# High and low parts of the weight chunks interleaved word by word in one tile

## The chip, the cores and the metric

The kernel runs on one core of one Trainium2 chip. The metric is the device time of one execution in microseconds (us). A core has TensorE (PE in the rows: matmuls; PEld: the loads of its stationary operand, the weights), VectorE (DVE), ScalarE (ACT), GpSimd (POOL) and SyncE (SP), which issues most of the transfers. The engines run on their own instruction streams and meet at semaphores.

## The reference, cut to what matters

One layer of a decoder for 256 prompt positions and 8 sample positions that share the weights, in float32:

```
h = RMSNorm(x);  [qA,kA,vA,qB,kB,vB] = h @ w_in              # 2048 -> 4352
oA = sliding window attention, oB = dilated window attention
x += RMSNorm(concat(RMSNorm(oA), RMSNorm(oB)) @ w_out)       # 2048 -> 2048
h = RMSNorm(x)
u = h @ w_gate;  up = h @ w_up                               # 2048 -> 5632, twice
y = (gelu(causal_conv3(u)) * up) @ w_down                    # 5632 -> 2048
x += RMSNorm(y)
```

The products with the five weight matrices matter here. They read 190.8 MB of weights once.

## The kernel before, in words

The 264 positions (`TOK`) lie along the free dimension, the features along the 128 partitions. Weights are the stationary operand and arrive in 364 chunks of 128 x 1024 floats (512 KB): 68 of `w_in`, 32 of `w_out`, 176 of `w_gate` and `w_up`, 88 of `w_down`. Everything goes through a ring of four slots (`RING`):

- SyncE loads chunk n into `raw[:, slot]` (`load`, line 360), once chunk n - 4 has been split by VectorE.
- ScalarE copies it to `wh[:, slot]` (`split`, line 424). The tile has the type fp32r, so this cast rounds to the high part. It waits for the chunk, and until TensorE is done with chunk n - 4.
- VectorE writes the low part, `wl = raw - wh` (`split`, line 681), once the cast is done.
- TensorE multiplies. `mm3` (lines 1130 to 1132) makes each product of three matmuls: high weight by high activation, high weight by low activation, low weight by high activation. Each has 128 stationary columns and 264 moving columns, and each loads its weights anew. A chunk has eight such products, 24 matmuls. `gemm` calls `mm3` for `w_in`, `w_out`, `w_gate` and `w_up`, `down` for `w_down`.

The activations are split in the same way: `hh` and `hl`, in the attention stage also `oBh` and `oBl`, for the last product `gh` and `gl`. They are the moving operand.

The order of work is written out by hand. In the attention stage (chunks 0 to 83) a table `PLAN` sets the attention's steps between the chunks: scores, masks, exponentials, transposes (line 1219) and products. Then comes the second half of `w_out`, then a loop over 22 rounds of 8 chunks for `w_gate` and `w_up`, called the FFN loop here: TensorE fills two banks with `u` and two with `up`; VectorE moves `u` to `U` (lines 912 and 913), subtracts chunks, adds the taps of the convolution (line 922), takes `up` (line 937), multiplies (940) and makes `gl` (943); ScalarE makes the first tap, the gelu (635 and 636) and `gh` (640). The last stage runs over `w_down` in two halves of 44 chunks. The first chunk is cast and split in two halves (lines 563 and 566, 849 and 853), so that TensorE can begin earlier.

Of the kernel before, what the change touches and what calls it, by code (L numbers as in the profile page):

```python
# [22 lines left out]
F32R = mybir.dt.float32r  # L23
# [4 lines left out]
P = 128  # L28
# [13 lines left out]
CH = 1024  # L42
RING = 4
# [146 lines left out]
def build(nc, d):  # L190

    ctx = ExitStack()
    with ctx:
# [3 lines left out]
        def sb(name, shape, dt=F32, into=ctx):  # L197
            return into.enter_context(nc.sbuf_tensor(name, shape, dt))
# [1 line left out]

        xT = sb("xT", [P, MT, TOK])
        raw = sb("raw", [P, RING, CH])
        wh = sb("wh", [P, RING, CH], F32R)
        wl = sb("wl", [P, RING, CH], F32R)
        par = sb("par", [P, N_PAR])
        ident = sb("ident", [P, P])
        ones = sb("ones", [P, P])
# [1351 lines left out]
```

## Time and profile before

| | |
|---|---|
| three timed runs | 1193.79, 1193.95, 1194.48 us, median 1193.95 |
| profiled execution, its own time | 1196.02 us |
| its span, first to last instruction | 1194.2 us |
| mean granted TensorE clock | 0.992 of full |
| busy: TensorE, weight loads | 98%, 95% |
| busy: VectorE, ScalarE, GpSimd | 58%, 46%, 9% |
| read from memory | 216.45 MB, 185 GB/s over the span |

Matmuls are pipelined and overlap in the records, so a matmul that "takes" 285 ns can start 122 ns after the one before. The pace of TensorE is therefore the length of a window divided by the number of matmuls in it. The weight load of a matmul runs while the matmul before it still streams. The durations of VectorE and ScalarE instructions are those of the engine's work, with a fixed part for each instruction.

### The profile page before, as it was taken

Reading aid. Unit: us, or ns where it says so; the run is one execution under the profiler, and the core shown is the slowest. Engines: PE = TensorE matmul, PEld = TensorE weight load, DVE = VectorE, ACT = ScalarE, POOL = GpSimd, SP = SyncE. Lnnn points to the kernel's source line nnn. Section 1 sums busy time; section 2 is a strip of 40 time slices with the busy share of each in tenths; the row PEclk is TensorE's granted clock in tenths of the full one; section 3 lists DMA queues with packets and bytes.
Section 4 is the critical chain, followed back from the end, with each engine's and each line's share of the span. In section 5 each row is a group of like instructions: output and inputs, shape, how many; then the busy total and the mean of one; then the engine's idle time right before and its main releaser. Section 6 shows DMA issues by size and latency. Waiting matters only on the chain.

```text
span 1194.2 us, 25575 instructions
## 1 busy us (share of the span) xinstructions
PE 1168.1 (98%) x9947; PEld 1135.4 (95%) x9947; DVE 698.4 (58%) x1050; ACT 554.4 (46%) x859; POOL 105.8 (9%) x163
## 2 busy tenths in 40 slices
PE   9999999999999799999999999999999999999995
PEld 8999889988899799999999999999999999999995
DVE  5877565674375865655656565656565444454445
ACT  7455555565455654444444443444444433343331
POOL 0100111110002010011001000100110000020001
PEclk9999999999999899999999999999999999999998
DMA  8746677676555345555465555555555655555551
GB/s 309 208 142 226 235 252 235 213 228 234 168 172 180 107 144 193 180 178 183 162 201 168 191 157 196 168 184 170 182 181 182 205 182 176 178 184 183 177 158 72
DMA packets 59473, 222.21 MB, mean 186 GB/s; under 512 B 7064, under 2 KB 7264, under 8 KB 57312
## 3 DMA queue, kind: packets, MB, share of 16 engines
q1 hardware_dynamic: 55152, 196.58, 51.2%
q0 software_dynamic: 4272, 24.94, 6.2%
q8 instruction: 35, 0.57, 0.2%
q14 instruction: 14, 0.11, 0.0%
HBM read 216.45 MB, written 5.00 MB: 185 GB/s over the span
## 4 chain that ended last, share of the span: by engine, by line
PE 93%; DVE 3%; DMA 2%; ACT 1%; issue 1%; SPq 0%; POOL 0%; DVEq 0%; ACTq 0%
PE ps L1130 29%; PE ps L1131 29%; PE ps L1132 28%; PE ps L1301 1%; DMA Vk<-in_vb 1%; PE ps L1219 1%; DVE wl L681 1%; PE ps L1282 1%; DMA xT<-in_x 1%; PE ps L1210 1%; PE ps L1208 1%; PE ps L1237 0%; PE ps L1155 0%; DVE yT L977 0%; DVE ps L976 0%
## 5 line engine op out<-in xcount | busy, mean ns | idle before, releaser
L1130 PE MATMUL ps<-hh,wh 128*128 128x264 f32 x2080 | 600.1, 289 | 8.2 <-DVE hl L886 5.8
L1132 PE MATMUL ps<-hh,wl 128*128 128x264 f32 x2080 | 593.0, 285 | 0.0
L1131 PE MATMUL ps<-hl,wh 128*128 128x264 f32 x1952 | 557.7, 286 | 0.0
L681 DVE TENSOR_TENSOR wl<-raw,wh 128x1024 fp32r<-128x1024 f32 x363 | 438.4, 1225 | 192.2 <-ACT wh L424 191.7
L424 ACT CAST wh<-raw 128x1024 fp32r<-128x1024 f32 x363 | 374.6, 1046 | 275.4 <-PE ps L1132 272.0
L1130 PEld LDWEIGHTS ps<-hh,wh 128*128 128x128 f32 x2080 | 394.0, 189 | 20.5 <-issue 17.5
L1132 PEld LDWEIGHTS ps<-hh,wl 128*128 128x128 f32 x2080 | 392.8, 189 | 0.0
L1131 PEld LDWEIGHTS ps<-hl,wh 128*128 128x128 f32 x1952 | 368.7, 189 | 0.1
L1131 PE MATMUL ps<-gl,wh 128*128 (+1 forms) x704 | 200.4, 285 | 0.0
L1130 PE MATMUL ps<-gh,wh 128*128 (+1 forms) x704 | 200.1, 284 | 0.0
L1132 PE MATMUL ps<-gh,wl 128*128 (+1 forms) x704 | 199.6, 283 | 0.0
L1130 PEld LDWEIGHTS ps<-gh,wh 128*128 128x128 f32 x704 | 132.5, 188 | 0.9 <-issue 0.9
L1131 PEld LDWEIGHTS ps<-gl,wh 128*128 128x128 f32 x704 | 132.6, 188 | 0.0
L1132 PEld LDWEIGHTS ps<-gh,wl 128*128 128x128 f32 x704 | 132.4, 188 | 0.0
L1096 POOL COPY co<-U 128x4 f32 (+1 forms) x22 | 21.2, 964 | 423.1 <-DVE U L913 423.1
L912 DVE TENSOR_TENSOR U<-ps,rB 128x512 f32<-128x512 f32 x22 | 15.2, 691 | 73.2 <-PE ps L1132 73.2
L630 ACT ACTIVATE cv<-U,par 128x280 f32<-128x280 f32 x44 | 25.0, 617 | 63.5 <-DVE U L913 63.5
L937 DVE TENSOR_TENSOR up<-ps,rB 128x528 f32<-128x528 f32 x21 | 14.9, 707 | 67.8 <-PE ps L1132 67.8
L640 ACT CAST gh<-up 128x528 f32 (+1 forms) x22 | 14.0, 634 | 73.0 <-DVE up L940 72.9
L922 DVE SCALAR_TENSOR_TENSOR cv<-U,par,cv 128x280 f32<-128x280 f32 x88 | 41.0, 506 | 9.9 <-ACT cv L630 6.8
L1130 PE MATMUL ps<-oBh,wh 128*128 128x264 f32 x128 | 37.6, 294 | 0.0
L1131 PE MATMUL ps<-hh,wh 128*128 128x264 f32 x128 | 36.5, 285 | 0.0
(229 smaller groups left out, 832.5 us busy)
## 6 DMA issues: line engine op xcount, KB each, us to landing
raw<-in_w_gate SPq DMA_DIRECT2D x88, 512.0 KB, 3.7
raw<-in_w_up SPq DMA_DIRECT2D x88, 512.0 KB, 4.6
raw<-in_w_down SPq DMA_DIRECT2D x88, 512.0 KB, 3.5
raw<-in_w_in SPq DMA_DIRECT2D x67, 512.0 KB, 4.8
raw<-in_w_out SPq DMA_DIRECT2D x32, 512.0 KB, 3.8
Kt<-in_kb POOLq DMA_DIRECT2D x8, 1284.0 KB, 6.2
Vk<-in_vb POOLq DMA_DIRECT2D x8, 1024.0 KB, 7.1
out_y<-yT SPq DMA_DIRECT2D x8, 264.0 KB, 2.1
```

The costliest lines, as they stand in the source:

```text
L424: nc.scalar.copy(wh[:, slot], raw[:, slot]).then_inc(hi_ready, 1)
L630: nc.scalar.activation(cv[:, k], U[:, k, 0:NU - 2], ACT.Identity, scale=par[:, bass.ds(i * 2 + (C_CW + k), 1)], bias=par[:, bass.ds(i * 2 ...
L640: nc.scalar.copy(gh[:, bass.ds(i * 2, 2)], up[:]).then_inc(gh_ready, 1)
L681: V.tensor_tensor(wl[:, slot], raw[:, slot], wh[:, slot].bitcast(F32), ALU.subtract).then_inc(lo_ready, 1)
L912: line.do(V.tensor_tensor(U[:, :, 2:2 + SEQ], ps[:, g:g + 2, 0:SEQ], wide(rB[:, 0:SEQ]), ALU.mult))
L922: ins = V.scalar_tensor_tensor(cv[:, k], U[:, k, tap:tap + NU - 2], par[:, bass.ds(i * 2 + (C_CW + FT * tap + k), 1)], cv[:, k], ALU.mult, ...
L937: V.tensor_tensor(up[:], ps[:, 2:4, 0:TOK], wide(rB[:]), ALU.mult).then_inc(up_taken, 1)
L1096: line.do(G.tensor_copy(co[:, bass.ds(i * 2, 2), 0:2], U[:, :, SEQ:SEQ + 2]))
L1130: nc.tensor.matmul(out, a, x, start=start, stop=False)
L1131: nc.tensor.matmul(out, a, xl, start=False, stop=False)
L1132: return nc.tensor.matmul(out, b, x, start=False, stop=stop)
L1208: nc.tensor.matmul(ps[:, B_S + h, 0:P], q[:, 0:P], k[:, 0:P], start=True, stop=True)
```

## The change

The tiles `wh` and `wl`, of four slots by 1024 words each, become one tile `whwl` with the last dimension 2, and `wh` and `wl` are now names of its even and its odd words. The tile has the bytes of the two before. All that reads or writes them stays as it is written: the casts write every second word, the subtractions read every second word and write the others, and each weight load reads 128 words, every second one of 256. `raw` and the activations stay contiguous.

```diff
--- before.py
+++ after.py
@@ -200,8 +200,8 @@
 
         xT = sb("xT", [P, MT, TOK])
         raw = sb("raw", [P, RING, CH])
-        wh = sb("wh", [P, RING, CH], F32R)
-        wl = sb("wl", [P, RING, CH], F32R)
+        whwl = sb("whwl", [P, RING, CH, 2], F32R)
+        wh, wl = whwl[:, :, :, 0], whwl[:, :, :, 1]
         par = sb("par", [P, N_PAR])
         ident = sb("ident", [P, P])
         ones = sb("ones", [P, P])
```

The instructions that touch them, before and after alike:

```python
nc.scalar.copy(wh[:, slot], raw[:, slot]).then_inc(hi_ready, 1)                       # 424
V.tensor_tensor(wl[:, slot], raw[:, slot], wh[:, slot].bitcast(F32), ALU.subtract)    # 681
a, b = wh[:, slot, c:c + P], wl[:, slot, c:c + P]                                     # mm3
```

## Rows read from the trace of the kernel before

**Rows 1.** The page: busy time by engine, and the chain that ended last.

```profile
PE 1168.1 (98%) x9947; PEld 1135.4 (95%) x9947; DVE 698.4 (58%) x1050; ACT 554.4 (46%) x859; POOL 105.8 (9%) x163
...
PE 93%; DVE 3%; DMA 2%; ACT 1%; issue 1%; SPq 0%; POOL 0%; DVEq 0%; ACTq 0%
PE ps L1130 29%; PE ps L1131 29%; PE ps L1132 28%; PE ps L1301 1%; DMA Vk<-in_vb 1%; PE ps L1219 1%; DVE wl L681 1%; PE ps L1282 1%; DMA xT<-in_x 1%; PE ps L1210 1%; PE ps L1208 1%; PE ps L1237 0%; PE ps L1155 0%; DVE yT L977 0%; DVE ps L976 0%
```

**Rows 2.** Groups by line and form: name, shapes, count, busy us, mean ns, idle before.

```profile
L681 DVE TENSOR_TENSOR wl<-raw,wh 128x1024 fp32r<-128x1024 f32 x363 | 438.4, 1225 | 192.2 <-ACT wh L424 191.7
L1130 PEld LDWEIGHTS ps<-hh,wh 128*128 128x128 f32 x2080 | 394.0, 189 | 20.5 <-issue 17.5 <-DVE wl L681 1.8 <-DVE vT L693 1.1
...
L424 ACT CAST wh<-raw 128x1024 fp32r<-128x1024 f32 x363 | 374.6, 1046 | 275.4 <-PE ps L1132 272.0 <-DMA raw<-in_w_in 2.6 <-ACT ge L650 0.3
...
L1219 PEld LDWEIGHTS ps<-ident,Sm 128*128 128x128 f32 x96 | 11.5, 140 | 0.0
...
L1301 PEld LDWEIGHTS ps<-Vk,pT 128*32 128x32 f32 x256 | 6.7, 109 | 3.5 <-DMA Vk<-in_vb 2.3 <-issue 1.2
...
L853 DVE TENSOR_TENSOR wl<-raw,wh 128x512 fp32r<-128x512 f32 x1 | 0.7, 692 | 1.1 <-ACT wh L566 1.1
...
L566 ACT CAST wh<-raw 128x512 fp32r<-128x512 f32 x1 | 0.6, 619 | 1.0 <-DMA raw<-in_w_in 1.0
```

**Rows 3.** Windows: us, busy (instructions) of each engine, granted clock, DMA share, GB/s.

```profile
36.00:200.00 164.00, 163.44 (x1545) 149.63 (x1546) 111.67 (x284) 84.63 (x197) 18.14 (x40) 1.00 0.66 214
450.00:750.00 300.00, 300.00 (x2451) 300.00 (x2451) 179.49 (x219) 132.37 (x167) 27.84 (x39) 1.00 0.55 180
850.00:1150.00 300.00, 300.00 (x2464) 300.00 (x2463) 145.31 (x141) 118.11 (x129) 14.89 (x14) 1.00 0.58 182
392.90:403.20 10.30, 5.50 (x25) 5.53 (x26) 10.13 (x16) 5.11 (x10) 0.00 (x0) 0.50 0.05 14
```

**Rows 4.** Timeline, clock at 0.5: start us, us, engine, line, tiles, count, idle before.

```profile
397.70 0.56 PE L1130 MATMUL ps<-hh,wh 128*128 128x264 f32 x1 [5.75 <-DVE hl L886]
...
398.06 0.42 PE L1131 MATMUL ps<-hl,wh 128*128 128x264 f32 x1
...
398.28 0.42 PE L1132 MATMUL ps<-hh,wl 128*128 128x264 f32 x1
```

**Rows 5.** Timeline of the weight loads around one transpose of `Sm`.

```profile
93.47 0.36 PEld L1219 LDWEIGHTS ps<-ident,Sm 128*128 128x128 f32 x3
```

**Rows 6.** Groups by form: short instructions with a step of three, and their long neighbours.

```profile
L912 DVE TENSOR_TENSOR U<-ps,rB 128x512 f32<-128x512 f32 x22 | 15.2, 691 | 73.2 <-PE ps L1132 73.2
...
L635 ACT ACTIVATE ge<-cv 128x512 f32<-128x512 f32 x22 | 13.9, 633 | 26.1 <-DVE cv L922 26.1
...
L636 ACT ACTIVATE ge<-cv 128x16 f32<-128x16 f32 x22 | 4.5, 207 | 0.0
...
L913 DVE TENSOR_TENSOR U<-ps,rB 128x16 f32<-128x16 f32 x22 | 3.7, 170 | 0.0
```

**Rows 7.** Timeline of the start.

```profile
10.30 1.23 DVE L681 TENSOR_TENSOR wl<-raw,wh 128x1024 fp32r<-128x1024 f32 x1 [0.96 <-ACT wh L424]
...
11.58 0.39 PE L1130 MATMUL ps<-hh,wh 128*128 128x264 f32 x1 [0.40 <-DVE wl L681]
```

**Rows 8.** Timeline of VectorE in one round of the FFN loop.

```profile
568.49 0.71 DVE L937 TENSOR_TENSOR up<-ps,rB 128x528 f32<-128x528 f32 x1 [3.31 <-PE ps L1132]
569.23 0.71 DVE L940 TENSOR_TENSOR up<-up,ge 128x528 f32<-128x528 f32 x1
570.92 0.71 DVE L943 TENSOR_TENSOR gl<-up,gh 128x528 f32 x1 [0.99 <-ACT gh L640]
...
580.34 0.69 DVE L912 TENSOR_TENSOR U<-ps,rB 128x512 f32<-128x512 f32 x1 [3.66 <-PE ps L1132]
580.94 0.17 DVE L913 TENSOR_TENSOR U<-ps,rB 128x16 f32<-128x16 f32 x1
...
582.58 2.01 DVE L922 SCALAR_TENSOR_TENSOR cv<-U,par,cv 128x280 f32<-128x280 f32 x4 [0.34 <-ACT cv L630]
```

## The prediction

> **What bounds the kernel now.** I read the page first, then the windows, then the groups of instructions by form, then short stretches of the timeline. TensorE is busy for 98% of the span, and the chain that ended last is 93% TensorE, with 29, 29 and 28% on the three matmul lines 1130, 1131 and 1132 [rows 1]. These are the three products of `mm3`: high weight by high activation, high weight by low activation, low weight by high activation. There are 364 chunks of 24 such matmuls, 8736 in all. VectorE is busy 58%, ScalarE 46% [rows 1], and both spend their time mostly in the two splitting instructions: the cast of a chunk, 363 times 1046 ns, and the subtraction, 363 times 1225 ns [rows 2].
>
> What the reader should take from the windows is the pace of TensorE: from 450 to 750 us it issues 2451 matmuls in 300 us, 122.4 ns each, and from 850 to 1150 us 2464, 121.8 ns each, both at the full granted clock [rows 3]. Two shorter times lie under that pace. In the one stretch with a granted clock of 0.5 (1.2 GHz, after TensorE had waited 5.75 us for `hl`), matmuls of the same form start 0.22 us apart [rows 4]; at double that clock the same 264 columns would take 0.110 us. And a weight load takes 0.83 ns a column, (189 - 109) / (128 - 32) from the loads of 128 and of 32 columns [rows 2], so 107 ns for 128; the three loads for a transpose, back to back, last 0.36 us, which at 140 ns for one [rows 2] is (0.36 - 0.14) / 2 = 0.11 us from start to start [rows 5]. So the load runs under the matmul before it and has at most some 13 ns to spare. The profile does not say which of the two makes the pace 122 instead of 110. That is the thin place of this change.
>
> **The change, part by part.** *Instructions.* None is added, removed or moved; every engine has the same instructions in the same order and the tiles take the same bytes. The sum therefore has only terms for the rate at which a step of two words (8 bytes) is read or written. The stream of matmuls that reads `hh`, `hl`, `gh`, `gl` keeps its step of one.
>
> *Weight loads, 8736 of them, on the path.* No row shows a load with a step. Lower bound of the cost: zero. The moving side of TensorE reads 264 columns of 4 bytes in at most 122.4 ns, 8.6 bytes per ns and partition, from the same memory [rows 3]. A load with a step of two passes over 128 x 8 bytes in 107 ns, 9.6 bytes per ns, words skipped included, and that is the rate of the moving side without its 12 ns (1056 bytes in 110 ns). So if the load's read path can do what the moving one does, skipped words are free. Upper bound: a column costs twice as much, 213 ns a load, and the load is then the bound: (213 - 122) x 8736 = 795 us. A gain I don't expect: the load is not shorter in any reading. I take zero, because the nearest row, the moving read, is within a few per cent of the rate needed.
>
> *Subtractions on VectorE, 363, and casts on ScalarE, 363.* The slopes are (1225 - 692) / 512 = 1.04 ns an element for VectorE and (1046 - 619) / 512 = 0.83 ns for ScalarE [rows 2]. Now the cast writes with a step of two, the subtraction reads one source and writes with it. Nearest rows: line 913 writes `U` with a step of three words, 16 elements, in 170 ns. The line through 512 elements (691 ns, line 912) at the slope above leads to 691 - 496 x 1.04 = 175 ns for 16 elements; doubled elements would add 17 ns. Line 636 on ScalarE reads `cv` with a step of three, 16 elements, in 207 ns, where 633 - 496 x 0.83 = 221 is the line [rows 6]. Neither shows a price, though 16 elements are few. Upper bound: elements cost double, 1225 + 1067 = 2.29 us and 1046 + 854 = 1.90 us. I take zero. What hides a small price: TensorE uses a chunk for 24 x 122 = 2.93 us, and the waits of the two engines are long, 191.7 us of VectorE for the cast and 272.0 us of ScalarE for TensorE [rows 2].
>
> *Start.* Up to about 20 us some casts and subtractions are themselves in the chain, for example the wait of `wl` on the cast and of TensorE on `wl` [rows 7]. At the taken price nothing changes; at double it costs about three subtractions and two casts, 3 x 1.07 + 2 x 0.85 = 5 us.
>
> Sum: 0. The profiled execution took 1196.02 us, 1194.2 of it span; the three timed runs have the median 1193.95, 2.07 less. No term gives a difference, so the forecast is that median, 1194.
>
> There is a rule that speaks against this change. The Trainium skill, "Vector Engine (DVE) Microarchitecture Reference", section 5.2, says that a port of VectorE runs at full rate only where its consecutive elements come in runs of two or more adjacent words, and gives 1.7 to 2.5 ns a column where elements hop singly. By it the subtraction would be about 1.9 to 2.7 us, an estimate. The row of line 913 speaks against it, with the shortness named. The skill's "SBUF — State Buffer", "Specifications (TRN2)", says otherwise: 16-byte lines, full bandwidth with two accesses in each, which a step of two words gives; the sum by that is zero. No run here has a long stepped access yet.
>
> **The rivals.** *VectorE pays double (slower, decided at 2.2 us a subtraction).* One round of the FFN loop is 8 chunks, 192 x 122.4 ns = 23.5 us. From a release of `U`, VectorE works 0.69 + 0.17 on `U`, 2.01 on the taps, 0.71 + 0.71 on `up`, waits 0.99 for ScalarE, 0.71 on `gl` [rows 8], 5.99 us, and eight subtractions. These fit while 8 s + 6.0 < 23.5, s < 2.19 us. With 2.29 a round takes 24.3 us: 0.8 us lost x 20 rounds = 16 us. Busy VectorE would be 179.49 + 102 x 1.07 = 289 of 300 us there, and 111.67 + 42 x 1.07 = 157 of 164 us in the attention stage [rows 3], where it also waits for scores; I put 10 us there, and 5 at the start. Together 31, so 1225. In the down stage 145.31 + 103 x 1.07 = 256 of 300 fits. For it: a wider step has to cost somewhere. Against: lines 913 and 636.
>
> *The load and the moving stream get in each other's way (slower).* The 12.4 ns between 110 and 122.4 may be stalls of reads that meet. When a load passes over twice the bytes, these can double: 12.4 x 8736 = 108 us, so 1302; a tenth of it is already 11 us. For it: the pace is above both floors and no wait explains it. Against: with three or more engines at work the pace hardly moves (122.4 with VectorE 60% busy, 121.8 with 48%).
>
> *The load pays per column (much slower).* 1194 + 795 = 1989; partial prices start to count after 13 ns a load, 12% of it. Against: the rate of the moving side.
>
> *A little faster.* The layout shifts which addresses meet, and a pace of 121.8 everywhere instead of 122.4 gives 0.6 x 5000 = 3 us, so 1191. Nothing in the profile asks for it.
>
> **How the numbers follow.** No effect 0.60 (1192 to 1196); VectorE or ScalarE pays 0.10 (1205 to 1245); reads meet 0.12 (1197 to 1302); the load pays per column 0.12 (1300 to 1990); a little faster 0.06 (1188 to 1191). The range from 1190 to 1245 leaves out the fourth case, the upper half of the third and a part of the last, 0.2 together. About 0.2%, 2.4 us, is what a measurement of this kernel can tell from no change. Same 0.60, slower 0.34, faster 0.06.
>
> **What would show it.** Right: loads of 128 columns at 189 ns, some 2451 matmuls in 300 us of the FFN, cast and subtraction at 1046 and 1225 ns. First rival: the subtraction above 2.2 us, TensorE waiting for it in the FFN loop. Second: the pace between 123 and 135 ns with loads of 189 ns. Third: loads of 230 ns and more, with the casts as before. The forecast is wrong if the step costs TensorE more than the 13 ns it can hide; no row of before can exclude that.

## The result, and the profile after

The changed kernel takes 1199.16 us, median of 20 runs; beside it the kernel before took 1193.78 us, median of 20. The ratio is 1.0042, with a 95% interval of 1.0036 to 1.0048: 5 us slower. The forecast was 1194.0 us, no change; the time lies inside the range of 1190 to 1245, on the side that had a chance of 0.34.

The profiled execution took 1199.3 us, with a span of 1197.5 us, 3.3 us more than before. Its page, the chain that ended last (compare [rows 1]):

```profile
PE 93%; DVE 3%; DMA 1%; ACT 1%; issue 1%; SPq 0%; POOL 0%; DVEq 0%; ACTq 0%
PE ps L1130 29%; PE ps L1131 29%; PE ps L1132 29%; PE ps L1301 1%; DMA Vk<-in_vb 1%; PE ps L1219 1%; DVE whwl L681 1%; PE ps L1282 1%; DMA xT<-in_x 1%; PE ps L1210 1%; PE ps L1208 1%; PE ps L1237 0%; PE ps L1155 0%; DVE yT L977 0%; DVE ps L976 0%
```

TensorE carries the chain as it did. The two splitting instructions and the loads, by line and form (compare [rows 2]):

```profile
L681 DVE TENSOR_TENSOR whwl<-raw,whwl 128x1024 fp32r<-128x1024 f32 x363 | 439.6, 1229 | 199.7 <-ACT whwl L424 199.1
L424 ACT CAST whwl<-raw 128x1024 fp32r<-128x1024 f32 x363 | 410.8, 1148 | 257.4 <-PE ps L1132 255.9 <-DMA raw<-in_w_in 0.8 <-ACT ge L650 0.3
...
L1130 PEld LDWEIGHTS ps<-hh,whwl 128*128 128x128 f32 x2080 | 407.6, 196 | 21.4 <-issue 18.7 <-DVE whwl L681 1.5 <-DVE vT L693 1.1
```

Everything that has a step of two now takes a little longer, and in very different measure. The subtraction goes from 1225 to 1229 ns. The cast goes from 1046 to 1148 ns, 10% or 0.10 ns an element. The weight load goes from 189 to 196 ns. What ScalarE waits for TensorE went down by 16 us, from 272.0 to 255.9: that is where part of its longer casts (36 us busy) went, and VectorE waits 199.1 instead of 191.7 us for them.

The windows show where TensorE lost its time (columns as in [rows 3]). First before, the one stretch of the attention stage that the prediction did not use:

```profile
60.00:180.00 120.00, 120.00 (x1146) 109.43 (x1145) 80.58 (x204) 62.38 (x146) 11.59 (x26) 1.00 0.66 215
```

The same stretches after:

```profile
60.00:180.00 120.00, 120.00 (x1141) 109.50 (x1140) 80.59 (x203) 65.99 (x149) 10.69 (x24) 1.00 0.65 211
450.00:750.00 300.00, 300.00 (x2452) 300.00 (x2451) 179.32 (x219) 142.23 (x165) 27.46 (x39) 1.00 0.54 180
850.00:1150.00 300.00, 300.00 (x2443) 300.00 (x2443) 143.95 (x140) 125.94 (x128) 14.89 (x14) 1.00 0.57 180
```

In the FFN loop the number has not changed, 2452 matmuls against 2451. In the third window there are 2443 in 300 us against 2464, 122.8 ns each instead of 121.8: 21 x 122.8 = 2.6 us lost in this window. It is not the stage of `w_down` alone: that stage begins at 921 us, so the first 71 us still belong to the FFN loop, and both means are mixed. In the attention stage 1141 stand against 1146, with a granted clock of 1.00 in both. The start times in the records say it more sharply. Count the matmuls of the program from 0. From matmul 7900 to 9600, all in the stage of `w_down`, 206.74 us became 209.09, 121.61 and 123.00 ns a matmul; from 4000 to 7600, in the FFN loop, both kernels take 441.00 us, 122.50 ns a matmul. Counted over the pairs of matmuls that follow each other without a wait in both kernels, the longer pace costs 1.3 us before the FFN loop, 0.1 or less in the FFN loop, 2.8 us in the stage of `w_down`: 4.1 us. This count comes from one pair of profiled executions, whose spans differ by 3.3 us; the medians of 20 differ by 5.4. The rest of 1.3 us is not placed.

### The profile page after: what moved, and what is told of

It reads as the page before. It is cut to its first block, busy times and chain, and to the rows that moved or that the text cites. A ratio compares the mean times of both kernels' runs of the same rounds, so it can differ in the third digit from the quotient of the medians.

```text
span 1197.5 us, 25575 instructions
## 1 busy us (share of the span) xinstructions
PE 1171.8 (98%) x9947; PEld 1139.3 (95%) x9947; DVE 699.8 (58%) x1050; ACT 590.5 (49%) x859; POOL 106.1 (9%) x163
## 4 chain that ended last, share of the span: by engine, by line
PE 93%; DVE 3%; DMA 1%; ACT 1%; issue 1%; SPq 0%; POOL 0%; DVEq 0%; ACTq 0%
PE ps L1130 29%; PE ps L1131 29%; PE ps L1132 29%; PE ps L1301 1%; DMA Vk<-in_vb 1%; PE ps L1219 1%; DVE whwl L681 1%; PE ps L1282 1%; DMA xT<-in_x 1%; PE ps L1210 1%; PE ps L1208 1%; PE ps L1237 0%; PE ps L1155 0%; DVE yT L977 0%; DVE ps L976 0%
## 5 line engine op out<-in xcount | busy, mean ns | idle before, releaser
L1130 PE MATMUL ps<-hh,whwl 128*128 128x264 f32 x2080 | 601.9, 289 | 9.0 <-DVE hl L886 5.8
L1132 PE MATMUL ps<-hh,whwl 128*128 128x264 f32 x2080 | 593.6, 285 | 0.0
L1131 PE MATMUL ps<-hl,whwl 128*128 128x264 f32 x1952 | 558.9, 286 | 0.0
L681 DVE TENSOR_TENSOR whwl<-raw,whwl 128x1024 fp32r<-128x1024 f32 x363 | 439.6, 1229 | 199.7 <-ACT whwl L424 199.1
L424 ACT CAST whwl<-raw 128x1024 fp32r<-128x1024 f32 x363 | 410.8, 1148 | 257.4 <-PE ps L1132 255.9
L1130 PEld LDWEIGHTS ps<-hh,whwl 128*128 128x128 f32 x2080 | 407.6, 196 | 21.4 <-issue 18.7
L1132 PEld LDWEIGHTS ps<-hh,whwl 128*128 128x128 f32 x2080 | 408.1, 196 | 0.0
L1131 PEld LDWEIGHTS ps<-hl,whwl 128*128 128x128 f32 x1952 | 382.2, 196 | 0.1
L1130 PE MATMUL ps<-gh,whwl 128*128 (+1 forms) x704 | 201.8, 287 | 0.0
L1131 PE MATMUL ps<-gl,whwl 128*128 (+1 forms) x704 | 201.2, 286 | 0.0
L1132 PE MATMUL ps<-gh,whwl 128*128 (+1 forms) x704 | 201.2, 286 | 0.0
L1130 PEld LDWEIGHTS ps<-gh,whwl 128*128 128x128 f32 x704 | 137.4, 195 | 0.9 <-issue 0.9
L1132 PEld LDWEIGHTS ps<-gh,whwl 128*128 128x128 f32 x704 | 138.1, 196 | 0.0
L1131 PEld LDWEIGHTS ps<-gl,whwl 128*128 128x128 f32 x704 | 137.8, 196 | 0.0
```

What stands on the lines that cost most here:

```text
L424: nc.scalar.copy(wh[:, slot], raw[:, slot]).then_inc(hi_ready, 1)
L681: V.tensor_tensor(wl[:, slot], raw[:, slot], wh[:, slot].bitcast(F32), ALU.subtract).then_inc(lo_ready, 1)
L1130: nc.tensor.matmul(out, a, x, start=start, stop=False)
L1131: nc.tensor.matmul(out, a, xl, start=False, stop=False)
L1132: return nc.tensor.matmul(out, b, x, start=False, stop=stop)
```

## The experiments

The theories at the outset: A, the loads with a step make the loss; B, the stepped casts and subtractions make it, by their traffic or by their length. All ratios are against runs of the kernel before on the same chip. Experiments 6 to 11 have one execution each and are read by their pace; their times in us were 2230.91, 1198.30, 1202.06, 1197.69, 1192.59 and 1196.35.

**1. One tile, everything contiguous.** The layout in which one side at a time can be given a step: in each half of a chunk the 512 high words and the 512 low words lie one after the other.

```diff
-        wh = sb("wh", [P, RING, CH], F32R)
-        wl = sb("wl", [P, RING, CH], F32R)
+        W = sb("W", [P, RING, 2, CH], F32R)
+        wh, wl = W[:, :, :, 0:CH // 2], W[:, :, :, CH // 2:CH]
-                a, b = wh[:, slot, c:c + P], wl[:, slot, c:c + P]
+                half, k = c // 512, c % 512
+                a, b = W[:, slot, half, k:k + P], W[:, slot, half, 512 + k:512 + k + P]
```

> High and low parts of half a chunk lie one after the other in one tile of the size of whwl; every read and write has a step of one. This is the layout in which the next two differ from before by one side only. If only the step matters, the time is that of before, ratio 0.999 to 1.001, casts 1046 ns, weight loads 189 ns, pace in the last stage 121.7 ns. If one tile or the addresses make the 0.42%, the time is already 1.003 to 1.005 of before.

Measured: 1194.8 us, ratio 1.0008 (0.9999 to 1.0016); casts 1046 ns, subtractions 1225 ns, loads 189 ns. In the stage of `w_down` it takes 206.74 us for the 1700 matmuls, as before. The tile and its addresses cost nothing that can be told.

**2. Only the loads have a step of two.**

```diff
-                a, b = W[:, slot, half, k:k + P], W[:, slot, half, 512 + k:512 + k + P]
+                a, b = W[:, slot, half, 2 * k:2 * k + 2 * P:2], W[:, slot, half, 2 * k + 1:2 * k + 2 * P:2]
```

> As e1_blocks_contig, but the weight loads read with a step of two while casts and subtractions write contiguous blocks (each load then gets a mix of high and low words: the products are not the reference's). Theory A, the loads make the loss: weight loads 196 ns, pace of the w_down stage 123.0 instead of 121.7 ns, time 1.002 to 1.005 of before, casts 1046 ns. Theory B, the stepped casts make it: loads may be 196 ns, but the pace stays 121.7 and the time within 0.999 to 1.001.

Measured: 1199.01 us, ratio 1.0037 (1.0024 to 1.0050). The groups and the windows of this kernel:

```profile
L1131 PEld LDWEIGHTS ps<-hh,W 128*128 128x128 f32 x2080 | 407.8, 196 | 20.5 <-issue 16.5 <-DVE W L681 1.7 <-DVE hl L844 1.1
...
L424 ACT CAST W<-raw 128x1024 fp32r<-128x1024 f32 x363 | 375.0, 1047 | 275.8 <-PE ps L1133 274.5 <-DMA raw<-in_w_in 0.6 <-ACT ge L650 0.3
```

```profile
60.00:180.00 120.00, 120.00 (x1141) 109.50 (x1141) 79.92 (x204) 62.38 (x146) 11.17 (x25) 1.00 0.65 213
450.00:750.00 300.00, 300.00 (x2451) 300.00 (x2451) 179.49 (x219) 132.23 (x166) 27.77 (x39) 1.00 0.54 180
850.00:1150.00 300.00, 300.00 (x2444) 300.00 (x2443) 144.19 (x141) 117.43 (x128) 14.91 (x14) 1.00 0.57 181
```

The loads take 196 ns, the casts 1047, and the windows are those of the changed kernel: 1141, 2451 and 2444 matmuls. The 1700 matmuls of the `w_down` stage take 209.09 us, the same as after to the last digit. This is theory A.

**3. Only the writes have a step of two.**

```diff
-        wh, wl = W[:, :, :, 0:CH // 2], W[:, :, :, CH // 2:CH]
+        wh, wl = W[:, :, :, 0:CH:2], W[:, :, :, 1:CH:2]
```

> As e1_blocks_contig, but the casts and subtractions write with a step of two as in the changed kernel, and the weight loads read contiguous words (products not the reference's). Theory A: casts 1148 ns, loads 189 ns, pace of the last stage 121.7 ns, time within 0.999 to 1.002. Theory B: the pace of the last stage rises to 123 ns, and the time is 1.003 to 1.005 of before, although the loads are contiguous.

Measured: 1194.47 us, ratio 1.0000 (0.9991 to 1.0009).

```profile
L681 DVE TENSOR_TENSOR W<-raw,W 128x1024 fp32r<-128x1024 f32 x363 | 439.8, 1229 | 199.0 <-ACT W L424 198.6
L424 ACT CAST W<-raw 128x1024 fp32r<-128x1024 f32 x363 | 408.8, 1143 | 255.1 <-PE ps L1133 253.8 <-DMA raw<-in_w_in 0.6 <-ACT ge L650 0.3
L1131 PEld LDWEIGHTS ps<-hh,W 128*128 128x128 f32 x2080 | 393.6, 189 | 21.7 <-issue 18.2 <-DVE W L681 1.3 <-DVE vT L693 1.1
```

```profile
850.00:1150.00 300.00, 300.00 (x2464) 300.00 (x2463) 145.38 (x141) 125.23 (x129) 14.91 (x14) 1.00 0.57 182
```

Casts are 1143 ns, loads 189, and the pace is that of before, 2464 in the window. The longer casts are real and fully covered. Theory B falls.

**4. A shorter moving stream.** What is the pace of 122.5 ns made of? In the kernel before, one of three matmuls gets 232 instead of 264 columns.

```diff
-                nc.tensor.matmul(out, a, xl, start=False, stop=False)
+                nc.tensor.matmul(out[:, 0:232], a, xl[:, 0:232], start=False, stop=False)
```

> The kernel before, with the second matmul of each product (high weight by low activation) over 232 of the 264 columns: the low activations of the last 32 positions are left out. It asks what makes the pace of 122.5 ns. If the moving stream makes it (264 columns at 0.417 ns and an overhead), every third matmul becomes 13 ns shorter, the mean pace falls by 4.4 ns to 118 ns in the FFN loop, and the time by about 3%. If the weight loads or the issue make it, the pace stays 122.5 ns and the time within 0.3% of before.

Measured: 1164.99 us, ratio 0.9751 (0.9737 to 0.9765).

```profile
450.00:750.00 300.00, 300.00 (x2535) 300.00 (x2534) 183.12 (x225) 136.39 (x170) 28.30 (x39) 1.00 0.56 186
850.00:1150.00 300.00, 300.00 (x2530) 298.58 (x2529) 143.27 (x139) 117.78 (x131) 13.07 (x11) 1.00 0.55 175
```

There are 2535 matmuls in the first window, 118.3 ns each; by the start times 118.47 in the FFN loop. The three matmuls of a product together take 3 x (122.50 - 118.47) = 12.1 ns less, or 0.38 ns for each column left out, where 0.417 was worked out from the stretch at half clock. So the moving stream makes the pace there. In the stage of `w_down` the start times give 118.57 instead of 121.61 ns, 9.1 ns for three or 0.28 ns a column: the larger part, but not all. From the start of the shortened matmul to the next it is 106.7 ns in the FFN loop and 107.5 in the stage of `w_down`, and the one behind it then takes 127.3 and 126.4 instead of 122.8 and 121.1: some of the gain is lost there, and why was not tested.

**5 and 6. A step of four and of eight words in the loads.** The parts of the half tile are read in another assignment; every word of it is still read once.

```diff
-                half, k = c // 512, c % 512
-                a, b = W[:, slot, half, 2 * k:2 * k + 2 * P:2], W[:, slot, half, 2 * k + 1:2 * k + 2 * P:2]
+                half, k = c // 512, c % 512 // P
+                k = 512 * (k % 2) + k // 2
+                a, b = W[:, slot, half, k:k + 509:4], W[:, slot, half, k + 2:k + 511:4]
```

> As e2_loads_step2, with a step of four words (16 bytes) in the weight loads, casts and subtractions contiguous; products not the reference's. If the cost grows with the bytes passed over, loads go from 189 and 196 (steps one and two) to some 203 to 210 ns, and the pace of the w_down stage from 121.6 and 123.0 to some 126 ns, time 1.01 to 1.02 of before. If every column then needs an access of its own at half the rate, loads take 189 + 107 = 296 ns or more and the time is 1.6 to 1.8 of before.

> As e5_loads_step4 with a step of eight words (32 bytes). If the price is one of accesses that share 16 bytes, it is that of step four; if it is one of bytes passed over, it is about double that of step four.

Measured: step four 2169.57 us, ratio 1.8169 (1.8139 to 1.8199); step eight 2230.91 us. With step four, the groups and a window of the FFN loop:

```profile
L1132 PEld LDWEIGHTS ps<-hh,W 128*128 128x128 f32 x2080 | 686.8, 330 | 18.3 <-issue 16.7 <-DVE W L849 0.9 <-DVE vT L740 0.4
```

```profile
700.00:1000.00 300.00, 300.00 (x1290) 298.85 (x1290) 96.14 (x116) 73.69 (x91) 14.38 (x21) 1.00 0.30 93
```

With step eight the load:

```profile
L1131 PEld LDWEIGHTS ps<-hh,W 128*128 128x128 f32 x2080 | 701.2, 337 | 17.4 <-issue 16.7 <-DVE vT L740 0.4
```

From step two to step four the load jumps from 196 to 330 ns, and the pace to 300 us / 1290 = 233 ns: now the load makes it. From four to eight there are only 7 ns more. So this isn't a price by bytes passed over. It has an edge between 8 and 16 bytes, behind which a column costs more than double ((330 - 189) / 128 = 1.10 ns more on 0.83); the changed kernel stands before it. A step of three words, 12 bytes, was not tried. The Trainium skill's page "SBUF — State Buffer", "Specifications (TRN2)", puts the edge there too: lines of 16 bytes, full bandwidth from two accesses in a line. By that rule a step of two keeps full bandwidth and a step of four does not; the runs agree on the edge, but not on a step of two for nothing: the load takes 7 ns more, the pace up to 1.4 ns, the cast 102 ns.

**7. Do the other engines disturb the loads?** The changed kernel with casts and subtractions cut to 8 words in the stage of `w_down`.

```diff
-                    nc.scalar.copy(wh[:, slot], raw[:, slot])
+                    nc.scalar.copy(wh[:, slot, 0:w], raw[:, slot, 0:w])                # w = 8 for w_down
```

> The changed kernel, with casts and subtractions of the w_down chunks cut to 8 of 1024 words (the last product is then not the reference's). If the 1.4 ns of the w_down stage come from loads that meet the stepped writes and reads of the other engines, the pace there falls from 123.0 to 121.6 ns or less. If they arise within TensorE's own two streams, it stays 123.0 ns.

Measured: 209.09 us for the 1700 matmuls, 123.00 ns, as in the changed kernel. The stepped work of the other two engines has no part in it. The transfers of weights have none either. In this run they fall at another time of a chunk (before and after, two thirds of the packets start 1.5 to 2.5 us into the 2.9 us of a chunk and 2% in its first 0.5 us; here 29% and 33%), and the pace is the same. And in the last chunks of `w_down` nothing moves any more, but the step costs what it did: in chunks 83 to 85 of the stage's 88, counted from 0, it costs 0.54, 1.50 and 0.79 ns a matmul; eight chunks earlier, with transfers, 0.54, 1.54 and 0.75. So the 1.4 ns arise within TensorE.

**8 and 9. Why in this stage and not in the FFN loop?** Two differences between the stages were taken away one at a time: the number of PSUM banks, and how often the moving tile changes.

```diff
-   ins = mm3(ps[:, (m + 4) % 8, 0:TOK], ..., gh[:, kt], gl[:, kt], first, last)
+   ins = mm3(ps[:, (m + 4) % 8 if first or last else 4 + m % 2, 0:TOK], ..., gh[:, kt], gl[:, kt], first, last)   # 8
+   x = kt - j + m // 2                                                                                            # 9
+   ins = mm3(ps[:, (m + 4) % 8, 0:TOK], ..., gh[:, x], gl[:, x], first, last)                                      # 9
```

> The changed kernel; the products of w_down between the first and the last chunk of a half go to two banks of PSUM in turn instead of eight, as in the FFN loop (sums not the reference's). It asks why the step costs 1.4 ns a matmul in the w_down stage and nothing in the FFN loop. If the banks make the difference, the pace is 122.5 ns, that of the FFN loop; if the order of the moving operands makes it, it stays 123.0 ns.

> The changed kernel; within a chunk of w_down the eight products take four activation tiles in turn, two products each, as in the FFN loop, instead of one tile for all eight (sums not the reference's). If the order of the moving operand is why the step costs 1.4 ns a matmul in this stage and nothing in the FFN loop, the pace goes from 123.0 to 122.5 ns. If it stays 123.0, neither banks nor moving order is the reason.

Measured, for the 1700 matmuls: two banks 209.09 us, 123.00 ns; moving order of the FFN loop 208.74 us, 122.79 ns. The number of banks does not move the stepped pace at all. The order moves it by 0.2 ns, less than the 0.5 that would lead to the pace of the FFN loop. What this leaves open is the other half of the comparison: the cost of the step is a difference to contiguous loads, and the same two edits were not made to the kernel before. If the order of the FFN loop alone raised the contiguous pace of this stage from 121.61 towards 122.5 ns, the step would cost almost nothing in it. So the moving order is not excluded as the reason.

**10 and 11. Is it the length of the load?** In the stage of `w_down` the loads take 96 of 128 columns, once in the kernel before, once in the changed one.

```diff
-   ins = mm3(ps[:, (m + 4) % 8, 0:TOK], (slot, P * m), gh[:, kt], gl[:, kt], first, last)
+   ins = mm3(ps[0:96, (m + 4) % 8, 0:TOK], (slot, P * m), gh[:, kt], gl[:, kt], first, last, 96)
```

> The kernel before; in the w_down stage the weight loads take 96 of 128 columns (a quarter of the outputs is left out). The load becomes 27 ns shorter, some 162 ns. If loads make part of the pace, it falls below 121.6 ns, at best to 110 to 113 ns. If only the moving stream and something fixed make it, it stays 121.6 ns.

> The changed kernel with the same cut in the w_down stage: loads of 96 columns with a step of two. If the 1.4 ns come from loads that are longer, the pace falls to that of e10; if they come from reads that meet while both streams run, a part of the difference to e10 stays, about 1 ns.

Loads of the kernel before, then of the changed one, in the stretch from 950 to 1130 us:

```profile
L1130 PEld LDWEIGHTS ps<-gh,wh 128*96 128x96 f32 x496 | 80.1, 161 | 0.0
```

```profile
L1130 PEld LDWEIGHTS ps<-gh,whwl 128*96 128x96 f32 x493 | 82.3, 167 | 0.0
```

| stage of `w_down` | load, contiguous | pace | load, step two | pace | difference |
|---|---|---|---|---|---|
| 128 columns | 189 ns | 121.61 ns | 196 ns | 123.00 ns | 1.39 ns |
| 96 columns | 161 ns | 121.26 ns | 167 ns | 122.01 ns | 0.75 ns |

The paces are again those of the 1700 matmuls. A load that is 28 ns shorter quickens the pace by 0.35 ns only, so its length is not the bound. And a stepped load of 167 ns, shorter than the contiguous one of 189, still goes with a slower pace, 122.01 against 121.61. The length of the load, the other engines and the transfers are thus excluded; what is left is that the step acts while the load and the moving stream run together, and at two lengths it does so more with more columns. What in TensorE they share was not shown.

**12. A step of four in the writes.** Loads contiguous, casts and subtractions at a step of 16 bytes.

```diff
-        wh, wl = W[:, :, :, 0:CH:2], W[:, :, :, 1:CH:2]
+        W4 = W[:].rearrange("p r h (c k) -> p r h k c", k=4)
+        wh, wl = W4[:, :, :, 0:2], W4[:, :, :, 2:4]
```

> As e3_writes_step2, but casts and subtractions write with a step of four words (16 bytes), loads contiguous (products not the reference's). If writes have the same edge as the loads between steps two and four, the cast goes from 1143 to about 1900 ns and the subtraction from 1229 to about 2300 ns, and the time is 1.01 to 1.05 of before. If the cast only pays by bytes passed over, it takes some 1240 to 1340 ns, the subtraction stays near 1230 ns, and the time is within 0.3% of before.

Measured: 1228.36 us, ratio 1.0282 (1.0265 to 1.0300).

```profile
L682 DVE TENSOR_TENSOR W<-raw,W 128x1024 fp32r<-128x1024 f32 x363 | 747.5, 2089 | 113.1 <-ACT W L425 112.5
L425 ACT CAST W<-raw 128x1024 fp32r<-128x1024 f32 x363 | 739.5, 2099 | 89.7 <-PE ps L1134 79.4 <-DMA raw<-in_w_up 6.2 <-DMA raw<-in_w_down 2.1
...
L1093 POOL COPY U<-par 128x32 f32 x21 | 40.2, 1914 | 36.3 <-DVE cv L923 36.3
```

```profile
450.00:750.00 300.00, 297.62 (x2425) 295.39 (x2424) 263.36 (x219) 231.78 (x168) 52.84 (x39) 1.00 0.56 175
850.00:1150.00 300.00, 299.90 (x2458) 299.71 (x2457) 236.97 (x155) 223.38 (x137) 31.48 (x20) 1.00 0.57 181
```

Who TensorE waits for now (us in total, times, longest):

```profile
PE ps L1132 <- DVE hl L887: 7.9, 4, 5.7
PE ps L1132 <- DVE W L682: 7.2, 12, 1.2
```

The same edge stands before the writes: the cast costs 2099 ns, double, and the subtraction 2089. VectorE is busy 263 of 300 us in the FFN loop, and TensorE still does only 26 matmuls less than 2451 there. By the start times the first 400 matmuls last 61.5 us instead of 53.7, matmuls 1600 to 3200 in the attention stage 175.4 instead of 164.8, the stretch around the norm, 3400 to 3600, 40.9 instead of 34.9. The first two rounds of the FFN loop, 3600 to 4000, lose 5.7 us, all that follows of it 0.8, the stage of `w_down` 0.5. The price is paid where the splitting is in the chain itself, and hardly in the steady loop.

## Why the prediction was right or wrong

*What bounds the kernel.* Right. TensorE's pace stayed the measure of everything; both thin places were named, and experiments 4 and 10 say which one it was: 32 moving columns less give 9.1 to 12.1 ns, a load 28 ns shorter gives 0.35.

*The weight loads.* The bounds held, but this term was put at nothing and was not nothing. It is the step that failed: "I take zero, because the nearest row, the moving read, is within a few per cent of the rate needed." The row shows 8.6 bytes per ns, 10% below the 9.6 that the stepped load needs; the two are equal only if the 12 ns between 110 and 122 are taken off, and no row said what those were. The term measures 1.4 ns in 122 in the stage of `w_down` (2.8 us), 0.6 ns in the attention stage (with the start and the norm 1.3 us) and nothing that adds up in the FFN loop, 4.1 us together, and 4.4 us by the ratio of experiment 2. A measurement of this kernel can tell 2.4 us, so zero in place of 0.5 to 1.1% of a matmul in two of the stages is what turned "same" into "slower". The upper bound, 213 ns a load and 1989 us in all, was not one for larger steps: step four has a pace of 233 ns and 2169.57 us.

*The casts and subtractions.* That they cost no time was right, one size was off. The subtraction costs 4 ns, as good as zero, and the cast 102 ns, where zero was taken from 16 elements at a step of three (line 636 reads, and does not write; a row for a stepped write of ScalarE was not there). Both are covered, as was said: experiment 3 has ratio 1.0000.

*The start.* No cost was forecast, and a small one is likely. In the kernels with the start of the changed one (after, experiments 7, 8, 9 and 11) the first 400 matmuls last 54.46, 53.99, 54.22, 53.54 and 54.01 us. Where loads or writes or both are contiguous (before, experiments 1, 2, 3 and 10) they last 53.66, 53.67, 53.62, 53.47 and 53.51. The means are 0.5 us apart, with one execution of each kernel and one that does not fit; it was not tested further.

*The rule that spoke against the change.* The page "Vector Engine (DVE) Microarchitecture Reference", section 5.2, has the Trainium skill ask for runs of two adjacent words; by that a subtraction would have been 1.9 to 2.7 us. Measured 1229 ns at a step of two, so at a step of two the rule does not hold here. At a step of four, 2089 ns, it does.

*The rivals.* "VectorE pays double" did not happen at a step of two. At a step of four it did, with 2089 ns just under the 2.19 us that were worked out as the point of decision: the FFN loop then keeps its pace to 0.2% (122.73 ns by the start times over matmuls 4000 to 7600), and the whole loses 34 us, where 31 had been priced. The sum fits better than its parts, which is luck: 16 us had been put on the FFN loop, 10 on the attention stage and 5 on the start, nothing on the norm. Measured were 6.5, 11.8 (matmuls 400 to 3400), 7.9 and 6.1. "The load and the moving stream get in each other's way" is the rival that the runs bear out, at 4.1 us of its full price of 108; the sign was a pace of 123 ns, and with it the loads were to stay at 189 ns, which they did not. Its argument against, that the pace hardly moves with other engines at work, was no argument: experiment 7 shows that other engines have no part in it. "The load pays per column" is what lies one step further.

*The chances.* They put 0.12 on the rival that happened. What could have moved them is in [rows 3]: two stages with paces of 122.4 and 121.8 ns and no wait between the matmuls. A pace that differs by 0.5% between stages with the same instruction forms may depend on how the reads fall, and then a change of how the reads fall can move it as well. This is an argument after the fact; what makes the two paces differ was not shown.

## What to carry to other kernels

A step of two float32 words is nearly free for VectorE (+0.3%), costs ScalarE's write 10%, and costs a TensorE whose loads run under full-rate moving streams up to 1% of its pace (0.4% of this kernel). A step of four words makes them 1.7, 2.0 and 1.9 times as long. So interleave two float32 streams if it saves more than that, and four only where neither side is near the bound: four in the writes cost 2.8% here, four in the loads 82%. Where TensorE is busy 98%, look at its pace by stage before and after a layout change: 0.4% of a kernel can sit in 1.4 ns of a matmul without a single wait in the profile.

## What the runs showed that was not expected

- The FFN loop keeps a pace of 122.50 ns, 441.00 us for 3600 matmuls, in all kernels with steps of one or two on both sides and full moving streams, though the load there is 7 ns longer as well; the stage of `w_down` does not. The cause stays open; moving order is not excluded, since experiments 8 and 9 have no partner with contiguous loads.
- That pace is a mean in which the step does show. By the start times, chunks of the FFN loop take 121.88 and 123.12 ns a matmul in turn with contiguous loads, and 122.62, 122.42, 122.29 and 122.67 in turn with stepped ones; the mean of four is 122.50 in both. In the stage of `w_down` the step costs between 0.4 and 2.9 ns a matmul, by chunk, in a pattern that comes back every eight chunks within 0.1 ns, but for the first chunks of each half. So what the step costs depends on a chunk's place in the order of work, and a single mean hides it.
- A load with a step of two takes 7 ns more for 128 columns and 5 or 6 ns for 96.
- With stepped casts and subtractions of 2.1 us, GpSimd's small copy of the conv state (line 1093) takes 1914 ns; in the kernel before the same copy, line 1092, took 1024 ns:

```profile
L1092 POOL COPY U<-par 128x32 f32 x21 | 21.5, 1024 | 49.7 <-DVE cv L922 49.7
```
